# A transformer kernel re-sequenced: mixer gates, the squares of the norms, attention's early passes, and the SGU's loads and variance

## The chip, the cores and the metric

The kernel runs on one core of one Trainium2 chip. A core has five engines that run at the same time, each through its own list of instructions in order: TensorE (PE, matrix products), VectorE (DVE), ScalarE (ACT), GpSimd (POOL) and SyncE (SP, which issues transfers here). They wait for each other on semaphores. The metric is device time in microseconds (us); lower is better.

## What is computed

Two stacks of layers, 1024 wide, one after the other on 512 tokens (528 in the first, with 16 extra ones):

```python
for l in range(2):                        # first stack, T = 528
    h = h + hybrid_mixer(rmsnorm(h, g), w_in[l], ..., w_out[l])
    h = h + conv_glu_ffn(rmsnorm(h, g), w_up[l], ..., w_down[l])
x = rmsnorm(h, final_norm_g)[:, 16:]
for i in range(2):                        # second stack, T = 512
    x = x + 0.5 * swiglu_ffn(rmsnorm(x, ...), ...)
    h = rmsnorm(x, mix_norm[i])
    x = x + (diff_attention(h) if i == 0 else chunked_sgu(h))
    x = x + 0.5 * swiglu_ffn(rmsnorm(x, ...), ...)

# hybrid_mixer: one input projection (26 column tiles of 128), three branches
o_hg  = rmsnorm(hgrn2(hq, hf, hi)) * silu(hg)            # 4 heads of 128
o_ret = groupnorm(retention(rq, rk, rv)) * silu(rg)      # 256 wide
o_lru = rg_lru(conv(lx)) * gelu(ly)                      # 256 wide
out   = concat(o_hg, o_ret, o_lru) @ w_out
# chunked_sgu (the gMLP): the layer norm is over the 2048 columns of v
u, v = split(gelu(h @ w_in + b_in)); v = layernorm(v)
s = w_s (8 groups, 128 x 128, causal) @ v + b_s;  out = (u * s) @ w_out + b_out
```

Everything is float32.

## The kernel before

Each float32 product is made of three fast ones (fp32r): high part by high part, low by high, high by low. Activations lie transposed in SBUF (128 features by T tokens). A projection is a list of **slabs** of weights: SP loads a slab as `raw`, ACT rounds it to `whigh` (line 774), POOL subtracts to get `wlow` (line 760), and PE multiplies. PE writes output tiles alternately into two slots of PSUM (`big`); semaphores `first_half` and `slab_done` say that a tile of slot 0 or 1 is done, `tile_out` that DVE has emptied it. All orders are written out by hand, engine by engine.

**Output projections** end in `residual()` (lines 1525 to 1560): for each of 8 output tiles, DVE adds the slot to `h` (line 1547 or 1544), makes the low part of the next layer's input (`low_of`, line 1457; its high part is ACT's, line 827), and adds the tile's squares (from ACT's Square, line 799) to `acc` for the next norm (`add_squares`, line 1407). The `final` norm has a second sum, `acc2`.

**The mixer** runs the HGRN2 in 9 half-chunks u; beside each, PE does a tile of the input projection (`tile(18 + u)`), `apply(u)`, `scores(u + 1)`, `to_tokens(u + 1)`, and after each second one `out_turn`. The gates are tiles 18 and 19 (`ret_gate`), 20 to 23 (`hg_gate`) and 24, 25 (`lru_gate`). ACT's Silu and Gelu need another function table than its exponentials (line 962), so each costs a table load. After the loop comes the first pass `outa` of the output projection, over the retention and LRU parts: its operand is `xhigh` (ACT, `operand_high`, line 1093) and `xlow` (DVE, `operand_low`, line 1886). The second pass `outb` is over the HGRN2 heads. The FFN follows.

**Attention** goes through units by half-steps h. From h = 48 on the first pass of its output projection, over the first EARLY heads, is woven in (`early_steps`): PE does 3 heads' steps per half-step (2 late on), and DVE's `partial_tile` (line 1513) adds a finished tile to `h` in the half-step after it. `outb` does the other heads.

**The gMLP** has phases gv and gu (v and u tiles), then token mixing `mix` (PE, line 2778) on the normalised `vtok`. POOL's queue begins gv with two transfers (lines 751, 754: `wraw`, `bs`). The variance is 8 ACT squares (line 1258) of v minus its mean, at u tiles 1 and 2; then DVE's root (`token_roots`, lines 1422 to 1430) and `token_norm` (line 2096), four operations per quarter.

## Time and profile before

| | |
|---|---|
| Time, median of 3 runs | 3527.51 us (3524.79 to 3528.49) |
| The profiled execution: its time, its span | 3526.83 us, 3525.0 us |
| PE busy | 3430.8 us, 97% |
| DVE, POOL, ACT busy | 1665.1, 1338.8, 1171.6 us |
| PE's granted clock, mean | 0.990 |
| HBM read | 290.93 MB |

The profiled execution lies 1.8 us outside its span (launch and end), and 0.7 us below the median. Busy times say how long an engine held an instruction; they overlap. A wait in the trace is written behind the instruction that it delays, with the idle time and what ended it.

### The profile page before, as it was taken

How to read it: one execution, taken by the hardware profiler on the slowest of the kernel's cores; microseconds unless marked ns; L12 is line 12 of the kernel's file. 1: busy time of each engine (PE TensorE's matmuls, PEld its weight loads, DVE VectorE, ACT ScalarE, POOL GpSimd, SP SyncE). 2: the span in 40 equal slices, each digit the busy share in tenths (PEclk: the TensorE clock that was granted, in tenths of full speed). 3: DMA queues.
4: the chain of work that ended last, by engine and by line, in shares of the span. 5: the costliest groups of instructions: out<-in, count | busy, mean ns of one | idle time of the engine just before them, and what ended most of it. 6: DMA issues, size and time to landing. Idle time of an engine off the chain costs nothing.

```text
span 3525.0 us, 54336 instructions
## 1 busy us (share of the span) xinstructions
PE 3430.8 (97%) x20190; PEld 2973.8 (84%) x20190; DVE 1665.1 (47%) x2642; ACT 1171.6 (33%) x1986; POOL 1338.8 (38%) x530
## 2 busy tenths in 40 slices
PE   7999999989989999999999989999999999999999
PEld 6998999989989898788877768888888877888887
DVE  5476534544765255532546754245423523734242
ACT  2465323324653233222235432222222234322122
POOL 3312443423134444444432224444444433344443
PEclk9999999999999999999999999999999999999999
DMA  3212332322123333233322113333333322233333
GB/s 107 73 43 61 89 92 88 93 66 69 43 66 90 96 88 97 78 101 90 99 74 61 61 48 95 96 93 98 90 95 90 101 86 83 78 92 93 95 95 96
DMA packets 561404, 294.91 MB, mean 84 GB/s; under 512 B 10727, under 2 KB 560230, under 8 KB 561142
## 3 DMA queue, kind: packets, MB, share of 16 engines
q1 hardware_dynamic: 560084, 291.33, 28.3%
q8 instruction: 91, 1.49, 0.2%
q0 software_dynamic: 768, 1.11, 0.1%
q10 hardware_dynamic: 418, 0.62, 0.1%
q14 instruction: 43, 0.35, 0.0%
HBM read 290.93 MB, written 2.10 MB: 83 GB/s over the span
## 4 chain that ended last, share of the span: by engine, by line
PE 62%; issue 26%; POOL 7%; DVE 3%; ACT 2%; POOLq 0%; DMA 0%; SPq 0%; ACTq 0%; DVEq 0%
PE big L2181 51%; POOL wlow L760 7%; PE big L2614 3%; PE big L2222 2%; PE misc L2235 1%; PE misc L2246 0%; PE misc L2668 0%; DVE mix_lev L1673 0%; PE misc L2272 0%; DVE fresh L1649 0%; ACT whigh L774 0%; PE misc L2778 0%; PE misc L2374 0%; PE big L2702 0%; DMA load_xin<-in_x 0%
## 5 line engine op out<-in xcount | busy, mean ns | idle before, releaser
L760 POOL TENSOR_TENSOR wlow<-raw,whigh 128x1024 fp32r<-128x1024 f32 (+2 forms) x508 | 1328.6, 2615 | 2158.4 <-ACT whigh L774 2158.4
L774 ACT CAST whigh<-raw 128x1024 fp32r<-128x1024 f32 (+2 forms) x508 | 563.4, 1109 | 1915.5 <-PE big L2181 1781.1
L2181 PE MATMUL big<-ffn_x2l,whigh 128*128 128x264 f32 (+2 forms) x2016 | 539.2, 322 | 0.0
L2181 PE MATMUL big<-ffn_x2h,whigh 128*128 128x264 f32 (+2 forms) x2016 | 536.9, 320 | 2.1 <-DVE ffn_zg L1585 2.1
L2181 PE MATMUL big<-ffn_x2h,wlow 128*128 128x264 f32 (+2 forms) x2016 | 536.4, 320 | 0.0
L2181 PE MATMUL big<-xhigh,whigh 128*128 128x512 f32 (+1 forms) x1680 | 525.3, 350 | 0.7 <-POOL wlow L760 0.7
L2181 PE MATMUL big<-xlow,whigh 128*128 128x512 f32 (+1 forms) x1680 | 518.3, 346 | 0.0
L2181 PE MATMUL big<-xhigh,wlow 128*128 128x512 f32 (+1 forms) x1680 | 516.2, 345 | 0.0
L2181 PE MATMUL big<-ffn_hidl,whigh 128*128 128x512 f32 (+1 forms) x1232 | 419.8, 364 | 0.0
L2181 PE MATMUL big<-ffn_hidh,wlow 128*128 128x512 f32 (+1 forms) x1232 | 418.7, 363 | 0.0
L2181 PE MATMUL big<-ffn_hidh,whigh 128*128 128x512 f32 (+1 forms) x1232 | 417.6, 362 | 0.0
L2181 PEld LDWEIGHTS big<-ffn_x2h,whigh 128*128 128x128 f32 x2016 | 335.4, 189 | 33.0 <-DVE ffn_zg L1585 2.5
L2181 PEld LDWEIGHTS big<-ffn_x2l,whigh 128*128 128x128 f32 x2016 | 335.1, 189 | 29.5
L2181 PEld LDWEIGHTS big<-ffn_x2h,wlow 128*128 128x128 f32 x2016 | 334.9, 189 | 28.6
L2181 PEld LDWEIGHTS big<-xhigh,whigh 128*128 128x128 f32 x1680 | 293.3, 189 | 45.0 <-POOL wlow L760 2.0
L2181 PEld LDWEIGHTS big<-xlow,whigh 128*128 128x128 f32 x1680 | 291.7, 189 | 39.2 <-issue 0.2
L2181 PEld LDWEIGHTS big<-xhigh,wlow 128*128 128x128 f32 x1680 | 291.7, 189 | 39.0
L1595 DVE TENSOR_TENSOR ffn_pr<-big,rstd 128x512 f32<-128x512 f32 x88 | 60.8, 691 | 417.0 <-PE big L2181 411.4
L2181 PEld LDWEIGHTS big<-ffn_hidh,whigh 128*128 128x128 f32 x1232 | 219.4, 188 | 40.6 <-DVE ffn_hidl L1605 0.5
L2181 PEld LDWEIGHTS big<-ffn_hidl,whigh 128*128 128x128 f32 x1232 | 219.6, 188 | 39.6
L2181 PEld LDWEIGHTS big<-ffn_hidh,wlow 128*128 128x128 f32 x1232 | 220.0, 188 | 37.9
L1603 DVE CAST ffn_hidh<-ffn_pr 128x512 f32 (+3 forms) x132 | 238.2, 1805 | 17.5
(402 smaller groups left out, 4090.7 us busy)
## 6 DMA issues: line engine op xcount, KB each, us to landing
raw<-in_ffn_w_gate_up SPq DMA_DIRECT2D x176, 512.0 KB, 3.8
raw<-in_ffn_w_down SPq DMA_DIRECT2D x96, 704.0 KB, 4.5
raw<-in_ffn_w_up SPq DMA_DIRECT2D x88, 512.0 KB, 3.8
raw<-in_w_in SPq DMA_DIRECT2D x52, 512.0 KB, 3.8
raw<-in_gmlp_w_in SPq DMA_DIRECT2D x32, 512.0 KB, 4.0
raw<-in_attn_w_in SPq DMA_DIRECT2D x24, 512.0 KB, 3.7
raw<-in_w_out SPq DMA_DIRECT2D x16, 512.0 KB, 3.5
raw<-in_gmlp_w_out SPq DMA_DIRECT2D x16, 512.0 KB, 3.6
```

The lines of the kernel that those rows point to most:

```text
L760: eng.tensor_tensor(wlow[:, at0:at0 + n], raw[:, at0:at0 + n], whigh[:, at0:at0 + n].bitcast(F32), ALU.subtract).then_inc(slab_split, 1)
L774: eng.copy(whigh[:, at0:at0 + w], raw[:, at0:at0 + w]).then_inc(high_rounded, 1)
L1595: eng.tensor_tensor(pr[:, 0:T], wide(big, 1, T), rstd[:, 0:T], ALU.mult).then_inc(tile_out[1], 1)
L1603: eng.tensor_copy(c1(hidh, i, K), pr[:, 0:K]).then_inc(hidh_ready, 1)
L2181: mm = eng.matmul(wide(big, slot, T)[:, c:c + n], w[:, (s * KC + k) * P:(s * KC + k + 1) * P], x[:, (x0 + k) * width + c:(x0 + k) * width ...
L2222: mm = eng.matmul(wide(big, s, T)[:, c:c + cn], w[:, (s * KC + k) * P:(s * KC + k + 1) * P], x[:, k * width + c:k * width + c + cn], start ...
L2235: mm = eng.matmul(dst[:, col + j * heads:col + (j + 1) * heads], src[:, x0:x0 + P], square(mat)[:, 0:P:P // heads], start=True, stop=True)
L2614: mm = eng.matmul(wide(big, j % 2, T2), w[:, (j % 2 * KC + k) * P:(j % 2 * KC + k + 1) * P], x[:, k * T1:k * T1 + T2], start=k == 0 and y ...
```

## The change

Five edits, in the order of the program:

1. **Mixer.** The LRU gate's tiles are now 20 and 21, those of the HGRN2 gate 22 to 25. ACT does the Gelu of the LRU gate right behind the Silu of the retention gate (u = 5), DVE multiplies by it one half-chunk earlier, and the four operands of outa are made together before `select`. PE does slab 0 of outa whole before `out_turn(3)`, and the `apply` of the last half-chunk stands between the two tiles of slab 1.
2. **Squares.** In `residual()` the squares of tile k - 1 are added after the residual of tile k.
3. **Attention.** EARLY is 4 instead of 5, the steps are spread two and three in turn, and `partial_tile` comes in the same half-step in which PE's tile is done.
4. **gv.** POOL makes the first pair of `wlow` before the two transfers.
5. **Variance.** v tiles 0 to 7 give a shift, and four squares of that half are done beside v tiles 11 to 14; the other four at u tiles 1 and 2. DVE has seven more small operations (`token_means`, one in `token_roots`).

```diff
-MIX_COLS = [(2048, 4), (2816, 2), (512, 4), (0, 4), (1024, 4), (2560, 2), (1536, 4), (3072, 2)]
+MIX_COLS = [(2048, 4), (2816, 2), (512, 4), (0, 4), (1024, 4), (2560, 2), (3072, 2), (1536, 4)]
-EARLY = 5
+EARLY = 4
-    counts = {h: 3 if h < 60 else 2 for h in range(48, ATT_END - 1)}
+    counts = {h: 2 + (h < 60 and h % 2 == 0) for h in range(48, ATT_END - 1)}
...
+                if st.name == "gv":
+                    pair(0)
+                    eng.wait_ge(slab_done, st.base)
...
+                    repeat(eng, 1, st.slabs // 2, pair)
+                    continue
...
-                    tile(18 + u)
+                    if u < LAST - 1:
+                        tile(18 + u)
+                    else:
+                        eng.wait_ge(slab_done, s0 + MIX_TILES)
+                        leave(eng.copy(c1(hg_gate, HH - 1), wide(big, 1, T1)), MIX_TILES - 1)
+                        for j in range(4):
+                            operand_high(j)
+                        high_of(s0 + MIX_TILES + 1)
...
                     if u == 5:
-                        for i in range(2):
+                        for i in range(4):
                             tile_wait(TILE_RG + i)
                         eng.activation(ret_gate[:, :], ret_gate[:, :], ACT.Silu).then_inc(gates_ready.sem, 1)
+                        eng.activation(lru_gate[:, :], lru_gate[:, :], ACT.Gelu_apprx_tanh).then_inc(gates_ready.sem, 1)
...
+                    if 11 <= i < 15:
+                        variance(0, i - 11)
...
-                        for k in range(4):
-                            variance(4 * (i - 1) + k)
+                        variance(1, 2 * (i - 1))
+                        variance(1, 2 * (i - 1) + 1)
...
+                        if more and not (isinstance(k, int) and k == 0):
+                            sums(k - 1, 1 - s)
...
-                        if more:
-                            add_squares(norm_of[m], k, s, Tn)
...
+                def sums(k, s):
+                    add_squares(norm_of[m], k, s, Tn)
...
+                if more:
+                    sums(KD - 1, 1)
...
-                eng.wait_ge(gates_ready.sem, gates_ready.at(l, "lru"))
-                for p in range(2):
-                    eng.tensor_tensor(c1(lh, p), c1(lh, p), c1(lru_gate, p), ALU.mult).then_inc(lgated.sem, 1)
-                operand_low(0)
-                operand_low(1)
+                        eng.wait_ge(gates_ready.sem, gates_ready.at(l, "lru"))
+                        for p in range(2):
+                            eng.tensor_tensor(c1(lh, p), c1(lh, p), c1(lru_gate, p), ALU.mult).then_inc(lgated.sem, 1)
+                for j in range(4):
+                    operand_low(j)
                 select(LAST)
...
-                        if done == h - 1:
+                        if done == h:
                             partial_tile(outa, T2, j, s)
...
                 for s in range(2):
                     slot_free(s, t1 // 2)
-                    for j in range(2):
+                    for j in range(4):
                         eng.wait_ge(x_ready, qo + j + 1)
-                        out_steps(0, s, [4 + j], j == 0, False, None)
+                        out_steps(0, s, [4 + j], j == 0, j == 3, slab_done if s else first_half)
                 out_turn(3)
...
+                out_steps(1, 0, [4, 5, 6, 7], True, True, first_half)
                 apply(LAST)
-                out_slab(outa, 1, [4, 5, 6, 7])
+                slot_free(1, t1 // 2 + 1)
+                out_steps(1, 1, [4, 5, 6, 7], True, True, slab_done)
```

In the lists below (rows of registers, branches and loop control are left out), names in front of the arrow are written, those behind it read.

**ACT at the end of a mixer.** In the half-chunk before the last, before the change, ACT's list has slab and gate copies, then the Gelu of the LRU gate with its table load, and the operands in two pairs (`mix_ro` retention, `mix_lh` LRU) around the norm of the output (lines 981 and 985):

```order
L774 CAST whigh<-raw 128x1024
L927 COPY mix_lru_gate<-big 128x528
L1104 ACT_TABLE_LOAD
L1104 ACTIVATE mix_lru_gate<-mix_lru_gate 128x1056
L1093 CAST xhigh<-mix_ro 128x528 x2
L981 COPY acc<-misc 128x256
L985 ACTIVATE mix_psel,mix_osum<-acc 128x128 x2
L1093 CAST xhigh<-mix_lh 128x528 x2
```

After the change the Gelu stands earlier, beside the Silu and before the exponentials (lines 964, 965):

```order
L1123 ACT_TABLE_LOAD
L1123 ACTIVATE mix_ret_gate<-mix_ret_gate 128x1056
L1124 ACT_TABLE_LOAD
L1124 ACTIVATE mix_lru_gate<-mix_lru_gate 128x1056
L964 ACT_TABLE_LOAD
L964 ACTIVATE fresh<-fresh 128x2x64
```

and where it stood there are a copy of the last gate tile and all four operands, in one piece:

```order
L1106 COPY mix_hg_gate<-big 128x528
L1095 CAST xhigh<-mix_ro 128x528 x2
L1095 CAST xhigh<-mix_lh 128x528 x2
L776 CAST whigh<-raw 128x1024
L983 COPY acc<-misc 128x256
L987 ACTIVATE mix_psel,mix_osum<-acc 128x128 x2
```

The Gelu and one more table load have moved ahead of the exponentials of the last half-chunk, and the norm's copies now stand behind all operands and a slab.

**DVE in the outb of a mixer**, the loop over its output tiles (two tiles per round), before:

```order
L1547 TENSOR_TENSOR h<-big,h 128x528
...
L1457 SCALAR_TENSOR_TENSOR ffn_x2l<-h,par,ffn_x2h 128x528
...
L1407 TENSOR_TENSOR acc<-acc,sqr 128x528
...
L1547 TENSOR_TENSOR h<-big,h 128x528
...
L1457 SCALAR_TENSOR_TENSOR ffn_x2l<-h,par,ffn_x2h 128x528
```

and after, with the peeled first round ahead of the loop and the last sum behind it:

```order
L1406 MEMSET acc 128x528
L1551 TENSOR_TENSOR h<-big,h 128x528
L1461 SCALAR_TENSOR_TENSOR ffn_x2l<-h,par,ffn_x2h 128x528
L1551 TENSOR_TENSOR h<-big,h 128x528
L1411 TENSOR_TENSOR acc<-acc,sqr 128x528
L1461 SCALAR_TENSOR_TENSOR ffn_x2l<-h,par,ffn_x2h 128x528
...
L1411 TENSOR_TENSOR acc<-acc,sqr 128x528
```

The sum of squares (`acc`) has moved from behind its own tile's low part to between the next tile's residual and low part.

**POOL at the start of the gMLP**, before, from the last slabs of the FFN ahead:

```order
L760 TENSOR_TENSOR wlow<-raw,whigh 128x1408
...
L760 TENSOR_TENSOR wlow<-raw,whigh 128x1408
...
L751 DMA gmw_wraw<-in_gmlp_w_s 128x8x128
L754 DMA gmw_bs<-in_gmlp_b_s 128x1024
...
L760 TENSOR_TENSOR wlow<-raw,whigh 128x1024
...
L760 TENSOR_TENSOR wlow<-raw,whigh 128x1024
```

and after:

```order
L752 TENSOR_TENSOR wlow<-raw,whigh 128x1408
...
L752 TENSOR_TENSOR wlow<-raw,whigh 128x1024 x2
L758 DMA gmw_wraw<-in_gmlp_w_s 128x8x128
L761 DMA gmw_bs<-in_gmlp_b_s 128x1024
...
L752 TENSOR_TENSOR wlow<-raw,whigh 128x1024
```

The first two `wlow` of the gMLP are ahead of the two transfers, which wait for the FFN's last tile.

## Rows read from the trace of the kernel before

**Rows 1.** Waits of the whole run on PE: us in all, times, longest us

```profile
PE big L2631 <- DVE h L1513: 8.1, 4, 3.9
PE big L2561 <- DVE xlow L1886: 7.2, 2, 3.6
...
PE big L2631 <- DVE h L1547: 3.1, 6, 0.7
...
PE big L2181 <- DVE ffn_zg L1585: 2.1, 2, 1.1
...
PE big L2631 <- issue: 1.0, 1, 1.0
PE big L2561 <- DVE h L1547: 1.0, 2, 0.5
...
PE big L2181 <- POOL wlow L760: 0.7, 1, 0.7
```

**Rows 2.** Timeline of PE, attention: start us, us, [idle before <-releaser]

```profile
2033.79 0.77 PE L2631 MATMUL big<-att_oh,whigh 128*128 128x512 f32 x1 [3.88 <-DVE h L1513]
...
2096.25 0.47 PE L2222 MATMUL big<-ffn_x2h,whigh 128*128 128x512 f32 x1 [1.27 <-issue]
...
2100.87 0.50 PE L2222 MATMUL big<-ffn_x2h,whigh 128*128 128x512 f32 x1 [1.61 <-POOL wlow L760]
```

**Rows 3.** Timeline of POOL at the start of the gMLP

```profile
2838.24 0.95 POOL L751 DMA_DIRECT2D gmw_wraw<-in_gmlp_w_s  x1 [10.92 <-PE big L2181]
...
2839.75 4.68 POOL L760 TENSOR_TENSOR wlow<-raw,whigh 128x1024 fp32r<-128x1024 f32 x2
```

**Rows 4.** Timeline of PE at the start of the gMLP

```profile
2842.16 0.80 PE L2222 MATMUL big<-xhigh,whigh 128*128 128x512 f32 x1 [4.22 <-POOL wlow L760]
2842.75 0.63 PE L2222 MATMUL big<-xlow,whigh 128*128 128x512 f32 x1
2843.18 0.63 PE L2222 MATMUL big<-xhigh,wlow 128*128 128x512 f32 x1
```

**Rows 5.** Timeline of PE at the start of an ordinary SwiGLU FFN

```profile
2471.23 0.50 PE L2222 MATMUL big<-xhigh,whigh 128*128 128x512 f32 x1 [0.84 <-POOL wlow L760]
2471.57 0.40 PE L2222 MATMUL big<-xlow,whigh 128*128 128x512 f32 x1
2471.80 0.39 PE L2222 MATMUL big<-xhigh,wlow 128*128 128x512 f32 x1
```

**Rows 6.** Timeline of ACT, gMLP: the first square of the variance

```profile
2960.17 1.15 ACT L1258 ACTIVATE sqr<-gm_vtok,gmo_vstat 128x1024 f32<-128x1024 f32 x1 [0.98 <-DVE gmo_vstat L2081]
```

**Rows 7.** Timeline of DVE, gMLP: root of the variance and two normalised quarters

```profile
2972.76 2.39 DVE L1426 SCALAR_TENSOR_TENSOR rcol<-rcol 128x4 f32<-128x4 f32 x1
...
2975.97 3.82 DVE L2096 TENSOR_SCALAR gm_vtok<-gm_vtok,gmo_vstat 128x512 f32<-128x512 f32 x4
...
2980.31 1.90 DVE L2096 TENSOR_SCALAR gm_vtok<-gm_vtok,gmo_vstat 128x512 f32<-128x512 f32 x4
```

**Rows 8.** Timeline of POOL beside it

```profile
2975.77 2.37 POOL L760 TENSOR_TENSOR wlow<-raw,whigh 128x1024 fp32r<-128x1024 f32 x1 [0.64 <-ACT whigh L774]
```

**Rows 9.** Timeline of PE, gMLP: first token mixing

```profile
2979.84 2.08 PE L2778 MATMUL misc<-gmo_wt,gm_vtok 128*128 128x128 f32 x8 [5.28 <-DVE gm_vtok L2096]
```

**Rows 10.** Timeline of ACT, end of mixer 0

```profile
263.14 1.09 ACT L1121 ACTIVATE mix_ret_gate<-mix_ret_gate 128x1056 f32<-128x1056 f32 x1
264.24 1.28 ACT L962 ACT_TABLE_LOAD   x1
```

**Rows 11.** Timeline of DVE, end of mixer 0

```profile
283.54 1.33 DVE L1905 TENSOR_TENSOR mix_lh<-mix_lh,mix_lru_gate 128x528 f32<-128x528 f32 x2 [4.62 <-ACT mix_lru_gate L1104]
```

**Rows 12.** Timeline of PE: mixer 0's output projection and its FFN

```profile
285.63 0.78 PE L2561 MATMUL big<-xhigh,whigh 128*128 128x264 f32 x2 [3.62 <-DVE xlow L1886]
...
343.69 0.52 PE L2222 MATMUL big<-ffn_x2h,whigh 128*128 128x264 f32 x2 [1.49 <-POOL wlow L760]
```

**Rows 13.** Windows: PE, PEld, DVE, ACT, POOL busy (x), PEclk, DMA share, GB/s

```profile
284.00:292.00 8.00, 6.37 (x32) 6.40 (x33) 5.07 (x11) 3.32 (x12) 0.00 (x0) 0.57 0.20 66
```

More of the change, by code:

```diff
@@ L1099, in mix @@
                         eng.wait_ge(lru_step.sem, lru_step.at(l, 1, 5))
-                    tile(18 + u)
-                    if u == LAST - 1:
-                        for i in (TILE_LY, TILE_LY + 1):
-                            tile_wait(i)
-                        eng.activation(lru_gate[:, :], lru_gate[:, :], ACT.Gelu_apprx_tanh).then_inc(gates_ready.sem, 1)
-                        operand_high(0)
-                        operand_high(1)
-                    out_copy(u)
-                    if u == LAST - 1:
-                        operand_high(2)
-                        operand_high(3)
-                    tokens(u + 1)
+                    if u < LAST - 1:
[6 more added lines that the diff above has]
+                        high_of(s0 + MIX_TILES + 1)
+                    out_copy(u)
+                    tokens(u + 1)
+                    if u == LAST - 1:
+                        out_scale(3)
                     if u % 2:
@@ L1233, in gmlp @@
                 t0, q0 = tile_of[n], fill_of[n]
-                mean, part, var2 = vstat[:, 0:4], vstat[:, 8:12], vstat[:, 16:24]
+                shift, var2 = vstat[:, 8:16], vstat[:, 16:24]
                 def gelu_tile(dst, slot, bias0, i, base):
@@ L1913, in mix @@
                 out_gate(1)
+                partial_tile(outa, To, 1, 0)
                 out_root(4)
-                partial(outa, To, 1)
+                partial_tile(outa, To, 1, 1)
                 out_low(0)
@@ L2058, in gmlp @@
                 t0, q0 = tile_of[n], fill_of[n]
-                mean, part, var, rs = [vstat[:, 8 * k:8 * k + 4] for k in range(4)]
-                var2 = vstat[:, 16:24]
+                mean, sums, shift, var2 = vstat[:, 0:4], (vstat[:, 4:8], vstat[:, 28:32]), vstat[:, 8:16], vstat[:, 16:24]
+                part, rs = vstat[:, 8:12], vstat[:, 24:28]
                 def scale_tile(st, i, at):
@@ L2073, in add_term, with token_means @@
                                              op0=ALU.mult, op1=ALU.add).then_inc(addend_ready, 1)
-                def token_means():
-                    eng.wait_ge(g_tok, NG)
-                    eng.tensor_reduce(part, vsum[:, :].rearrange("p (j m) -> p j m", j=4), AX.X, ALU.add).then_inc(g_mean, 1)
-                    eng.wait_ge(g_mean, 1)
-                    eng.tensor_scalar(mean, part, -1.0 / GH, None, ALU.mult).then_inc(g_mean, 1)
-                    eng.tensor_scalar(part, part, -float(GH) ** -1.5, None, ALU.mult).then_inc(g_mean, 1)
+                def token_means(half):
+                    eng.wait_ge(g_tok, 8 * (half + 1))
+                    v = vsum[:, :].rearrange("p (j m) -> p j m", j=4)[:, :, 8 * half:8 * half + 8]
+                    eng.tensor_reduce(sums[half], v, AX.X, ALU.add).then_inc(g_mean, 1)
+                    eng.wait_ge(g_mean, 3 * half + 1)
+                    eng.tensor_scalar(shift[:, 4 * half:4 * half + 4], sums[half], -2.0 * float(GH) ** -1.5, None, ALU.mult
+                                      ).then_inc(g_mean, 1)
+                    if half == 0:
+                        eng.tensor_copy(mean, sums[0]).then_inc(g_mean, 1)
+                        return
+                    eng.tensor_tensor(mean, sums[0], sums[1], ALU.add).then_inc(g_mean, 1)
+                    eng.tensor_tensor(sums[0], sums[0], sums[1], ALU.subtract).then_inc(g_mean, 1)
+                    eng.wait_ge(g_mean, 7)
+                    eng.tensor_scalar(mean, mean, -1.0 / GH, None, ALU.mult).then_inc(g_mean, 1)
+                    eng.tensor_tensor(sums[1], sums[0], sums[0], ALU.mult).then_inc(g_mean, 1)
@@ L2083, in token_roots @@
                 def token_roots():
                     eng.wait_ge(g_var, 8)
-                    eng.wait_ge(g_mean, 3)
-                    v2 = var2.rearrange("p (j x) -> p j x", x=2)
-                    eng.tensor_tensor(part, v2[:, :, 0], v2[:, :, 1], ALU.add).then_inc(g_root, 1)
+                    eng.wait_ge(g_mean, 9)
+                    eng.tensor_tensor(part, var2[:, 0:4], var2[:, 4:8], ALU.add).then_inc(g_root, 1)
                     eng.wait_ge(g_root, 1)
+                    eng.scalar_tensor_tensor(out=part, in0=sums[1], scalar=float(GH) ** -2, in1=part,
+                                             op0=ALU.mult, op1=ALU.add).then_inc(g_root, 1)
@@ L2131, in gmlp @@
                         add_term(2 * (i - 4) + 1)
+                    if i == 10:
+                        token_means(0)
                 eng.wait_ge(addend_ready, NG)
```

54 lines of the change are left out of this document (24 added, 30 removed).

## The prediction, made before the changed kernel ran

> **What bounds the kernel now.** I read the busy times first: PE holds an instruction for 97% of the span, and no edit adds or removes a matmul of any size. So the change can only gain what PE waits, and what it loses to a lower clock after a wait. Next comes the list of PE's waits by what ended them [rows 1]: the reader is to see that those which the edits touch are small. Then the timelines of PE around the longest of them, and of the engine that ended each. Last, the matmuls behind a long wait: at the gMLP's start they follow each other at 0.43 us [rows 4], against 0.23 us for the same matmul in an ordinary FFN [rows 5]. That is TensorE at the lower of its two clocks (1.2 of 2.4 GHz). A wait of 3 us or more on PE thus costs its length and some 2 to 3 us behind it; shorter ones mostly cost their length.
>
> **Attention and its FFN's start: -10.8 us (-6 to -14).** Waits for the residuals in this part are 8.1 us in 4 waits (line 1513, partial sums of the first pass), 1.0 us in one, and 3.1 us in 6 (line 1547) [rows 1]; with 1.27 and 1.61 at the FFN's first tiles [rows 2] that is 15.1 us. Two more are lost at the low clock behind the longest (3.88 us) [rows 2]: about ten matmuls of 512 columns at 0.43 instead of 0.23 us. After the change, four heads' steps instead of five make a tile, and DVE empties the slot in the half-step in which it is filled, so PE comes back to the slot with a half-step in between where it had none. I followed the semaphores through h = 48 to 64: six waits are left, of about 0.6, 0.6, 0.3, 2.85, 0.4 and 0.7 us, 5.5 in all. The long one is the residual of slot 1 at h = 54, which stands in DVE's order behind `combine` and `out_root`. That takes some 8.8 us off up to the end of outb (its six waits of 0.5 us stay at roughly a third, since the sum of squares, next paragraph, leaves the chain), and 2.0 at the FFN, where the second slab's subtraction comes earlier and an ordinary FFN's 0.84 us [rows 5] is left in place of 1.27 + 1.61. The ends: if two of the six are longer than I read them, -6; if the 2.85 us does not come, -14.
>
> **Squares one tile later: in the terms of each FFN start.** In an output loop the chain for a slot is PE's tile, DVE's residual, ACT's high part (0.9 us), DVE's low part, and then the squares, 0.7 us, ahead of the next residual. The edit puts them in the 0.9 us in which DVE waits for ACT anyway. No work is added. At the two mixers the waits that go are 0.5 us each in outb (1.0 in 2 on line 1547 [rows 1], and as much on "issue"), most of the 1.49 us behind POOL [rows 12], and the 1.1 us at the FFN's first gate (2.1 in 2, line 1585 [rows 1]). I take -2.9 and -3.0, **-5.9 us** in all (-3 to -6). At the starts of norms that wait on `acc` the last sum is where it was: 0 (0 to +0.7).
>
> **gv: -6.1 us (-5 to -6.5).** POOL waits for the last tile of the FFN before, issues two transfers, 2838.24 to 2839.75, and only then subtracts twice (4.68 us) [rows 3]; PE waits 4.22 us for the first [rows 4]. An ordinary FFN with its `wlow` ready waits 0.84 us [rows 5]. That is 3.4 us. Then about twelve matmuls at 0.43 instead of 0.23, 2.4 to 2.7 us more. The transfers land about 4 us later and are needed some 15 us after the start, so they stay hidden; if they didn't, PE would wait about 1 us.
>
> **Token mixing: -6.9 us (-1.9 to -8.2).** The first mixing waits 5.28 us [rows 9], and a tile just before it 0.7 [rows 1]; the low clock behind it costs 2.2 us (eight small matmuls at double time and six large ones). The wait is the sum of ACT's eight squares from 2960.17, of 1.15 us and the read of their sum, 1.3 each [rows 6], the root, and four normalisations [rows 7]. Four squares move to v, 5 us off ACT's chain; the seven new DVE operations are 0.2 us each, and six of them lie in idle time. Not all 5.3 us go, since DVE is held up twice here. A small root operation takes 2.39 us and four normalisations 3.82, against 1.90 for four a little later [rows 7], and each time POOL's subtraction, 2.37 us, starts in the same moment [rows 8]. One such hold-up stays in my reading, and about 1.3 us of wait. The Trainium skill says in "SBUF — State Buffer", section "Who interferes with whom", that VectorE and GpSimd share a port pair and whoever issues first holds it for its whole instruction; the trace agrees (2.39 us beside 2.37). By that rule alone, whether the next subtraction catches the last normalisation is decided by about 0.4 us, and this is the first rival.
>
> **Mixer ends: 0 us (-8 to +6, both mixers).** Before, outa's first matmul waits 3.62 us [rows 12] for the Gelu, the gating [rows 11] and the operands, and the clock in 284 to 292 is 0.57 [rows 13]: 3.6 us and some 2.8 more per mixer. In the new order the Gelu (1.09, as the Silu) and a table load (1.28) [rows 10] lie ahead of the exponentials of the last half-chunk, and the gating of 1.33 us [rows 11] ahead of its DVE work. That chain, exponentials, state, copies for the tokens, `apply`, has PE waiting for it: 2.4 + 1.3 = 3.7 us later, in three waits of about 2.1, 1.3 and 0.3. PE thus reaches outa at 285.5 instead of 285.63, now without a wait. The gain is the low clock, if three shorter waits do not bring it as well; the Silu of the HGRN2 gate comes at the same time as before and bounds outb's start, so that I find at most 0.9 us at each mixer, and 1.7 to 2.7 us of loss if the clock falls again. I take 0. The ends: the 3.7 us all hidden, -4 each; all exposed behind the old bound, +3 each. In "ScalarE: Activation LUTs", section "What ACT_TABLE_LOAD costs", the Trainium skill adds a drain of 1380 ns to the 1283 ns of a table load; here the load starts 0.01 us after the activation ahead of it ends and takes 1.28 [rows 10], so that the trace does not show it. By the page the estimate would be 2.8 us slower in all.
>
> **Sum.** -10.8 - 5.9 - 6.1 - 6.9 + 0 = -29.7 us. The profiled execution took 3526.8, 0.7 below the median of 3527.5; so 3497.1 on its own scale and 3497.8 on the median's. I say 3497.
>
> **Rivals.**
> - *The port.* DVE's last normalisation falls behind a second subtraction (2.4 us), the mixing waits 4.1 us and the low clock stays: the term is -1.9 instead of -6.9, 3502. The same at the output loops: a pair of tiles needs 4.7 us of DVE and, with a subtraction in it, 7.1, against 6.1 us of PE; the twelve slabs of three such loops lose up to 1.0 each: 3509. For it: both held-up operations in [rows 7]. Against it: PE waits only 0.5 us per tile in such loops now [rows 1]. Chance 0.2.
> - *The mixers lose.* The new waits bring the low clock before outa; +3 each and the FFN starts at the small end (-3): 3506. For it: the clock falls behind shorter waits too (the 0.57 of [rows 13] lasts longer than the wait). Chance 0.12.
> - *The mixers gain.* ACT has slack that I have not seen, and neither wait nor clock loss is left: -4 to -7 each, 3484 to 3489. Chance 0.1.
> - *The waits move only.* In attention DVE's order, not PE's slots, sets the pace; attention gives 4, the others half: 3527 - 15 = 3512. Chance 0.06.
> - *Slower.* One mechanism at the mixers: PE has nothing to do while the exponentials wait for Gelu and table, so the whole 3.7 us is exposed, and the clock stays low from there through outa, 24 us of work at half rate, up to 12 us: 15.7 each, 31 in both, 3528. It decides from 15 us per mixer on. Against it: in [rows 13] the low clock went after 6 us. Chance 0.02.
>
> The forecast has 0.5. A difference of 0.2%, 7 us, is about what a measurement of this kernel can tell from none. Faster by more than that: all cases but the last and the tail of the one before, 0.94; within it 0.04; slower 0.02. The range is that of the terms and takes in the port, the losing mixers and most of the gaining ones: 3484 to 3512.
>
> **What would show it.** Right: PE's waits on line 1517 (the new number of 1513) below 5 us in all, one of them near 2.9; the gMLP's first wait below 1 us with matmuls 0.23 apart behind it; the first mixing's wait at 1 to 2 us; no wait over 0.5 at outa, but three ahead of it. Wrong: a clock below 0.7 in 262 to 292, a mixing wait of 4 us with POOL's subtraction beside the last normalisation, low parts or residuals in outb that take 2 us and more one after another, or waits of PE in attention that keep their sum and change their name.

## The result and the profile after

The changed kernel takes 3507.73 us (median of 5 runs, 3507.09 to 3513.93) against 3527.35 us before: ratio 0.9951, 95% interval 0.994 to 0.9963, 19.6 us less. The forecast was 3497, 30 us less, with 3484 to 3512 as range. Time and sign lie inside it, but a third of the gain is missing, and the terms are off by more than the sum. The profiled execution took 3507.73 us, its span 3505.9; the spans of the two profiled executions differ by 19.1 us. The same marks of PE in both traces (the ends of waits that both have) divide that:

| mark (us) | before | after | gained since the last |
|---|---|---|---|
| first wait in mixer 0's half-chunk 6 | 256.78 | 256.00 | 0.8 |
| second slab of the FFN behind mixer 0 | 343.69 | 339.97 | 2.9 |
| the same wait in mixer 1 | 959.61 | 956.07 | -0.2 |
| second slab of the FFN behind mixer 1 | 1044.34 | 1039.48 | 1.3 |
| attention, last wait before the first pass | 1842.22 | 1837.56 | -0.2 |
| second slab of the FFN behind attention | 2100.87 | 2094.19 | 2.0 |
| second slab of the next FFN | 2471.23 | 2464.67 | -0.1 |
| end of the wait at the first token mixing | 2979.84 | 2962.61 | 10.7 |
| second slab of the last FFN | 3150.78 | 3131.69 | 1.9 |

The 0.8 us at the top are the first load, which ended earlier in that execution. The gMLP gives 10.7 + 1.9, the mixers 4.2, attention 2.0.

Such a stretch is exact for its two executions, but PE's clock falls in some executions of the same code and not in others, and each time that moves a mark by about 1.6 us. Two falls of this kind are in the table. The trace of the kernel before has a low clock right behind the first mark (0.52 in 257 to 260), which b_squares, with the same code there, has not (1.00): 1.6 of the mixers' 4.2 us are that. In attention it is the other way round. In 2045 to 2050 the clock of the kernel before is 1.00, but it fell there in the traces of c_mixer and d_gmlp, whose attention is the same code, and they take 630.6 us from attention's last wait to the second slab of the next FFN, where the kernel before takes 629.0. Against them attention gains 3.5 us, not 1.9.

The list of PE's waits after, in us in all, times and longest, with the rows that answer to [rows 1]:

```profile
PE big L2243 <- POOL wlow L752: 10.8, 8, 2.0
PE misc L2416 <- issue: 8.8, 6, 3.2
PE big L2652 <- DVE h L1517: 8.5, 4, 4.6
...
PE misc L2799 <- DVE gm_vtok L2115: 1.5, 1, 1.5
```

The 7.2 us on outa's operands are gone, and 5.3 at the token mixing are 1.5. But the partial sums of attention (line 1517, before 1513) are 8.5 us in 4 waits, where they were 8.1, and the mixers' line on "issue" has come up from 2.7 to 8.8. So PE waits for attention's partial sums as long as before. Its timeline there, against [rows 2]:

```profile
2036.31 0.47 PE L2652 MATMUL big<-att_oh,whigh 128*128 128x512 f32 x1 [2.03 <-DVE h L1517]
...
2045.70 0.80 PE L2652 MATMUL big<-att_oh,whigh 128*128 128x512 f32 x1 [4.55 <-DVE h L1517]
...
2064.40 0.51 PE L2652 MATMUL big<-att_oh,whigh 128*128 128x512 f32 x1 [1.61 <-DVE h L1517]
...
2094.19 0.50 PE L2243 MATMUL big<-ffn_x2h,whigh 128*128 128x512 f32 x1 [2.04 <-POOL wlow L752]
```

What DVE did ahead of each is in its timeline, and below it is POOL's for the same stretch:

```profile
2032.70 2.86 DVE L1448 TENSOR_TENSOR att_ol<-fresh,att_oh 128x512 fp32r<-128x512 f32 x1
...
2041.48 2.19 DVE L1427 TENSOR_SCALAR rcol<-rcol 128x4 int32<-128x4 int32 x1
...
2060.65 2.12 DVE L1429 TENSOR_TENSOR rcol<-rcol 128x4 f32<-128x4 f32 x1
```

```profile
2032.25 2.76 POOL L752 TENSOR_TENSOR wlow<-raw,whigh 128x1024 fp32r<-128x1024 f32 x1 [16.05 <-ACT whigh L776]
...
2041.31 2.34 POOL L752 TENSOR_TENSOR wlow<-raw,whigh 128x1024 fp32r<-128x1024 f32 x1 [6.30 <-ACT whigh L776]
...
2058.03 4.72 POOL L752 TENSOR_TENSOR wlow<-raw,whigh 128x1024 fp32r<-128x1024 f32 x2 [14.38 <-ACT whigh L776]
```

Three operations that take 0.68, 0.17 and 0.16 us elsewhere take 2.86, 2.19 and 2.12, and each ends where a subtraction of POOL ends (2032.25 + 2.76 = 2035.01, the DVE operation 2035.56 with 0.6 of its own; 2041.31 + 2.34 = 2043.65, the operation 2043.67; 2058.03 + 4.72 = 2062.75, the operation 2062.77). That is the hold-up of [rows 7, 8], in a stretch (2029 to 2072) in which the kernel before has none of it.

The gMLP, PE's timeline and then DVE's and POOL's, against [rows 4, 7, 9]:

```profile
2835.12 0.50 PE L2243 MATMUL big<-xhigh,whigh 128*128 128x512 f32 x1 [0.95 <-POOL wlow L752]
...
2962.61 1.16 PE L2799 MATMUL misc<-gmo_wt,gm_vtok 128*128 128x128 f32 x8 [1.46 <-DVE gm_vtok L2115]
```

```profile
2956.82 2.40 DVE L1427 TENSOR_SCALAR gmo_vstat<-gmo_vstat 128x4 int32<-128x4 int32 x1
...
2960.64 1.92 DVE L2115 TENSOR_SCALAR gm_vtok<-gm_vtok,gmo_vstat 128x512 f32<-128x512 f32 x4
...
2962.36 2.43 POOL L752 TENSOR_TENSOR wlow<-raw,whigh 128x1024 fp32r<-128x1024 f32 x1 [3.16 <-ACT whigh L776]
```

gv now begins without a wait, and its second slab waits 0.95 us, about as in every FFN. At that slab (2847.45 before, 2835.12 after) the two terms can be told apart: gv gives 5.8 us, the mixing 6.8. At the mixing one root operation is held up (2.40), the four normalisations are not (1.92), and PE waits 1.46 us.

The mixer's end, PE and ACT, against [rows 10, 12]:

```profile
271.01 0.66 PE L2416 MATMUL misc<-squares_sb,mix_v 128*128 128x128 f32 x2 [3.22 <-issue]
...
284.27 0.49 PE L2582 MATMUL big<-xhigh,whigh 128*128 128x264 f32 x2
```

```profile
264.41 1.08 ACT L1124 ACTIVATE mix_lru_gate<-mix_lru_gate 128x1056 f32<-128x1056 f32 x1
...
265.51 1.28 ACT L964 ACT_TABLE_LOAD   x1
```

Instead of the forecast three waits of 3.7 us in all there is one of 3.22, ahead of `to_tokens`. Outa starts at 284.27 without a wait, and the clock of 284 to 292 is not low, but it falls behind the new wait:

```profile
284.00:292.00 8.00, 8.00 (x68) 8.00 (x67) 3.83 (x8) 4.31 (x14) 2.40 (x1) 1.00 0.21 66
270.00:275.00 5.00, 3.99 (x22) 4.02 (x23) 3.72 (x15) 3.33 (x13) 2.36 (x1) 0.66 0.14 32
```

(The columns are those of [rows 13].) In mixer 0 the low clock has moved ahead of outa and is shorter there; in mixer 1 it has moved as well, and is as long as before (0.66 in 987 to 992 before and in 970 to 975 after).

### The profile page after: what moved, and what is told of

It is laid out like the page before. It is cut to its first block, busy times and chain, and to the rows that moved or that the text cites. A ratio compares the mean times of both kernels' runs of the same rounds, so it can differ in the third digit from the quotient of the medians.

```text
span 3505.9 us, 54254 instructions
## 1 busy us (share of the span) xinstructions
PE 3420.9 (98%) x20190; PEld 2965.9 (85%) x20190; DVE 1669.8 (48%) x2649; ACT 1171.2 (33%) x1986; POOL 1348.9 (38%) x530
## 3 DMA queue, kind: packets, MB, share of 16 engines
q8 instruction: 91, 1.49, 0.2%
## 4 chain that ended last, share of the span: by engine, by line
PE 61%; issue 29%; POOL 7%; DVE 2%; ACT 1%; POOLq 0%; DMA 0%; SPq 0%; DVEq 0%; ACTq 0%
PE big L2202 51%; POOL wlow L752 7%; PE big L2635 3%; PE big L2243 2%; PE misc L2256 1%; PE misc L2267 0%; PE misc L2689 0%; PE misc L2293 0%; PE misc L2799 0%; PE big L2723 0%; ACT whigh L776 0%; DVE fresh L1492 0%; PE misc L2307 0%; DVE acc L1411 0%; DMA load_xin<-in_x 0%
## 5 line engine op out<-in xcount | busy, mean ns | idle before, releaser
L752 POOL TENSOR_TENSOR wlow<-raw,whigh 128x1024 fp32r<-128x1024 f32 (+1 forms) x508 | 1338.7, 2635 | 2140.1 <-ACT whigh L776 2140.1
L776 ACT CAST whigh<-raw 128x1024 fp32r<-128x1024 f32 (+1 forms) x508 | 563.5, 1109 | 1907.4 <-PE big L2202 1776.9
```

Of the source, the lines that this page charges most:

```text
L752: eng.tensor_tensor(wlow[:, at0:at0 + n], raw[:, at0:at0 + n], whigh[:, at0:at0 + n].bitcast(F32), ALU.subtract).then_inc(slab_split, 1)
L776: eng.copy(whigh[:, at0:at0 + w], raw[:, at0:at0 + w]).then_inc(high_rounded, 1)
```

## The experiments

Twelve kernels ran, each beside the kernel before, whose median was between 3527.2 and 3528.4 in the same sessions. The changed kernel itself was timed only in its own session. "Against the changed kernel" thus compares sessions, and its interval (0.994 to 0.9963) touches or overlaps those of all the runs built on it but e_short, l_cut and m_cutnosq: a difference of a few us is not shown by the medians alone.

| run | edit | median us | ratio to before, 95% |
|---|---|---|---|
| a_att | before + attention edit | 3521.39 | 0.9984 (0.9974 to 0.9993) |
| b_squares | before + squares edit | 3532.04 | 1.0015 (1.0005 to 1.0024) |
| c_mixer | before + mixer edit | 3524.09 | 0.999 (0.9981 to 1.0) |
| d_gmlp | before + both gMLP edits | 3514.82 | 0.9965 (0.9953 to 0.9978) |
| e_short | after, short subtractions in attention | 3499.71 | 0.992 (0.9903 to 0.9937) |
| f_casts | after, roundings re-placed | 3504.12 | 0.9935 (0.9919 to 0.9952) |
| g_rootlast | after, partial sum ahead of the root | 3508.23 | 0.9946 (0.9929 to 0.9962) |
| h_castfirst | after, last rounding first | 3507.98 | 0.9942 (0.9926 to 0.9959) |
| j_nosq | after - squares edit | 3508.46 | 0.9945 (0.9928 to 0.9962) |
| k_best | j + f + g | 3502.06 | 0.9929 (0.9912 to 0.9945) |
| l_cut | after, short subtractions in second passes | 3492.82 | 0.9907 (0.9891 to 0.9924) |
| m_cutnosq | l - squares edit | 3493.49 | 0.9904 (0.9887 to 0.992) |

### The edits one by one

```diff
-EARLY = 5
+EARLY = 4
...
-                        if done == h - 1:
+                        if done == h:
```

> The kernel before with the attention edit alone (EARLY 4, steps two and three in turn, partial_tile in the same half-step). My theory, the port: POOL's subtractions of the output projection's slabs now start beside DVE operations that they hold up by about 2.2 us each, in the att_ol subtraction near h = 52 and twice in out_root; so this edit by itself brings 0 to -2 us (about 3526) and those three DVE operations take 2 to 3 us. Rival, the new order works as I had worked it out and something in the other edits spoils it: -8 to -9 us here (about 3518), with every DVE operation at its usual length.

> The kernel before with the squares edit alone. If the sum of squares is out of the slot's chain and nothing takes its place, the waits on the residuals in the three output loops go and -3 us comes in all from the two mixers and 2 from attention. With the port theory every second low part takes 2.5 us instead of 0.77, and the wait for the FFN's second subtraction grows from 1.5 to 1.9 us: -1 us per loop, -3 in all, 3524.

> The kernel before with the mixer edit alone. The wait of 3.6 us ahead of outa goes and one of 3.2 us for the state of the last half-chunk comes: 0 to -1 us per mixer, 3526. Rival, the two mixers' gain in the changed kernel (4.2 us) is this edit's and not the squares': -4 us, 3523.

> The kernel before with the two gMLP edits (subtractions ahead of the transfers, variance in two halves) alone. Both terms as in the changed kernel: -12.6 us, 3515, with no matmul at 0.43 us pitch at the start of gv or behind the first mixing. Rival: part of that gain needs the other edits (the phase of slabs and transfers): less than 10.

The four effects are -6.5, +4.2, -3.8 and -13.1 us on their own medians, -19.2 in all, beside 19.6 for the whole change. That they add up is partly chance: without the squares edit the other three make -23.4, and the kernel that has just these three (j_nosq, below) gains 18.7.

**a_att** came out between the two theories, and by its time (-2.5 to -9.2 us) the rival's -8 would be possible. Its trace has the hold-ups at the first and the last place (2.86 and 2.10 us), so that the rival is out, but not the one in the middle. As I read it the reason is PE's clock. After the same wait of 2.03 us it fell here and not in the changed kernel (PE's timeline and then the window behind the wait in a_att, and the window behind the same wait, at 2036.31, in the changed kernel; PEclk is the third column from the right):

```profile
2040.83 0.47 PE L2631 MATMUL big<-att_oh,whigh 128*128 128x512 f32 x1 [2.03 <-DVE h L1513]
```

```profile
2041.00:2046.00 5.00, 5.00 (x24) 4.69 (x24) 3.10 (x8) 1.63 (x4) 0.00 (x0) 0.61 0.31 103
```

```profile
2036.00:2041.00 5.00, 4.70 (x29) 4.02 (x29) 3.13 (x8) 2.82 (x6) 0.00 (x0) 1.00 0.38 105
```

With PE at half rate, ACT's copy and its rounding came later, POOL's subtraction began at 2047.67, behind the root instead of in it, and the 4.55 us wait is missing (timelines of POOL and DVE in a_att):

```profile
2047.67 2.39 POOL L760 TENSOR_TENSOR wlow<-raw,whigh 128x1024 fp32r<-128x1024 f32 x1 [8.14 <-ACT whigh L774]
...
2046.00 0.17 DVE L1423 TENSOR_SCALAR rcol<-rcol 128x4 int32<-128x4 int32 x1
...
2047.46 0.68 DVE L1513 TENSOR_TENSOR h<-big,h 128x512 f32<-128x512 f32 x1
```

So a fall of the clock saved the next, longer wait. The other traces bear this out. Behind the same wait of 2.03 us the clock fell in l_cut and m_cutnosq too (0.57 and 0.59 over 5 us), and neither has the long wait; it did not fall in h_castfirst and j_nosq (1.00), and both have it, 4.54 and 4.55. (It fell in g_rootlast as well, 0.55, but there DVE's order is another one.) From the same mark to the next FFN's second slab (1842 to 2466) a_att takes 624.2 us, and j_nosq, with the same code there, 627.2.

**b_squares** is the surprise: slower, and beyond what either theory had. The hold-ups are there, DVE and POOL in attention's second pass:

```profile
2081.78 2.34 DVE L1407 TENSOR_TENSOR acc<-acc,sqr 128x512 f32<-128x512 f32 x1
...
2087.60 2.27 DVE L1407 TENSOR_TENSOR acc<-acc,sqr 128x512 f32<-128x512 f32 x1
...
2094.36 2.47 DVE L1457 SCALAR_TENSOR_TENSOR ffn_x2l<-h,par,ffn_x2h  x1 [0.34 <-ACT ffn_x2h L827]
```

```profile
2081.72 1.85 POOL L760 TENSOR_TENSOR wlow<-raw,whigh 128x768 fp32r<-128x768 f32 x1 [7.27 <-ACT whigh L774]
...
2087.47 1.85 POOL L760 TENSOR_TENSOR wlow<-raw,whigh 128x768 fp32r<-128x768 f32 x1 [3.90 <-ACT whigh L774]
...
2093.43 2.85 POOL L760 TENSOR_TENSOR wlow<-raw,whigh 128x1024 fp32r<-128x1024 f32 x1 [4.10 <-ACT whigh L774]
```

ACT makes the high part, the square and the rounding of the next slab in one go, so POOL starts a little after each pair of tiles. In the old order the residual lay there, which reads one operand from PSUM and was not held up, and the 0.9 us in which DVE waits for ACT (DVE and POOL in the kernel before):

```profile
2080.32 0.69 DVE L1547 TENSOR_TENSOR h<-big,h 128x512 f32 x1
...
2080.17 1.92 POOL L760 TENSOR_TENSOR wlow<-raw,whigh 128x768 fp32r<-128x768 f32 x1 [7.37 <-ACT whigh L774]
```

With the sum moved, DVE has a sum (2.34, 2.27) or a low part (2.47) there in every round. But that alone is not the 4 us. PE's six waits of 3.1 us in the second pass are now three of 2.7, and the pass is 0.4 us shorter; the FFN's second slab then waits 2.04 us for POOL instead of 1.61. What follows is the clock, PE's window behind that slab in b_squares and, behind a wait of the same 2.04 us, in the changed kernel:

```profile
2103.00:2107.00 4.00, 4.00 (x12) 3.15 (x11) 0.67 (x2) 0.00 (x0) 0.00 (x0) 0.57 0.45 131
...
2094.00:2098.00 4.00, 3.81 (x21) 3.29 (x22) 1.29 (x2) 0.00 (x0) 0.14 (x1) 1.00 0.44 131
```

The fall costs 1.7 us. The clocks of all executions say the same: in b_squares's ten the mean is 0.988, in the 27 of the kernel before it is 0.990. The share that is missing to 1, times the span, is the most that a low clock can cost: 42.0 and 35.7 us, 6.3 us apart, where the medians are 4.2 apart. So all or most of its loss is one of clock. Which of its waits brings the falls is not shown, since the changed kernel has the same hold-ups in its second passes and loses nothing by the edit.

**c_mixer** gives -3.8 us, with an interval that reaches 0. It is nearer to the rival (-4) than to my 0 to -1 for each mixer, but it doesn't settle what the squares edit adds there: with the chance fall of the clock taken out the mixers' stretches of the changed kernel give 2.6 us, and those of c_mixer's trace, which has falls of its own, 2.1. **d_gmlp** is as forecast.

### Is it the port, and how much?

```diff
-                        at0, n = s * KC * P, st.kc * P
+                        at0, n = s * KC * P, 8 if st.name in ('aouta', 'aoutb') else st.kc * P
```

> The changed kernel, but POOL subtracts only 8 of the 1024 columns of each slab of attention's output projection (its low parts are left out of the product, so the output is not the reference's). Port theory: no DVE operation in 2024 to 2090 is held up any more (att_ol 0.7, root operations 0.2), the waits of 2.0, 4.6 and 1.6 us shrink to 0, about 2.4 and 0, the low clock behind the longest goes: -6 to -8 us against the changed kernel. Rival, DVE's order (out_root ahead of the partial sum) sets the waits: -1 us or less and the 4.6 us stays above 4.

PE's work is the same in this run; it multiplies by what `wlow` held before. It gives -8.0 us against the changed kernel, and 10.3 in the stretch from attention's last wait ahead of the first pass (1840.74) to the second slab of the next FFN but one (2457.56). In the first pass the hold-ups are gone and one wait of 2.45 us is left of the three; in the second, two low parts are still held up (2.33 and 2.43 us) by the subtractions for the FFN (timelines of DVE and of PE in e_short):

```profile
2034.83 0.69 DVE L1448 TENSOR_TENSOR att_ol<-fresh,att_oh 128x512 fp32r<-128x512 f32 x1
...
2041.44 0.17 DVE L1427 TENSOR_SCALAR rcol<-rcol 128x4 int32<-128x4 int32 x1
```

```profile
2043.64 0.51 PE L2652 MATMUL big<-att_oh,whigh 128*128 128x512 f32 x1 [2.45 <-DVE h L1517]
```

The 2.45 us are the partial sum behind the root, which I had worked out as 2.85 before the change ran; the clock did not fall behind them (1.00 in 2043 to 2048). The rival is out as the cause of the other two waits and of 2.1 of the 4.55 us; the order of DVE's work sets the rest.

### Can it be had with all the work done?

```diff
+                    if h == EARLY_DONE[0, 1] + 1:
+                        high_of(outa.base + 2)
...
+                    if h == EARLY_DONE[2, 1] + 1:
+                        high_of(outb.base)
...
-                        if EARLY_DONE[j, 1] == h - 1:
-                            high_of(outa.base + j + 2)
+                    if h == EARLY_DONE[1, 1] + 1:
+                        eng.wait_ge(tile_out[1], (t0 + 24) // 2 + 2)
+                        high_of(outa.base + 3)
+                    if h == EARLY_DONE[3, 1] + 1:
+                        eng.wait_ge(aorstd, AH)
+                        high_of(outb.base + 1)
```

> The changed kernel with ACT's four roundings in attention's output projection moved so that POOL's subtractions fall into DVE's idle time: the first ahead of the exponentials, the second and the fourth behind a wait for the partial sum and for out_root, the third ahead of out_head. All work is done. Port theory: as e_short, -5 to -8 us against the changed kernel. Rival: less than -1 us, since the hold-ups only ran beside a wait that stays; or the later slabs make PE wait for POOL and give back 2 us.

-3.6 us, and 4.7 in attention's stretch. All four executions (3502.9 to 3504.6) are faster than all five of the changed kernel. POOL's four subtractions take 2.37 or 2.38 us each. Behind the last three DVE's operations keep their usual time, so three of the four placings work, and the first does not (timelines of POOL, DVE and PE in f_casts):

```profile
2030.85 2.38 POOL L752 TENSOR_TENSOR wlow<-raw,whigh 128x1024 fp32r<-128x1024 f32 x1 [13.11 <-ACT whigh L776]
...
2046.08 2.37 POOL L752 TENSOR_TENSOR wlow<-raw,whigh 128x1024 fp32r<-128x1024 f32 x1 [12.85 <-ACT whigh L776]
...
2031.13 2.10 DVE L2000 TENSOR_TENSOR att_top<-att_top,att_alpha 128x2 f32<-128x2 f32 x1
```

```profile
2034.83 1.13 PE L2696 MATMUL misc<-att_kt,att_qt 64*128 64x512 f32 x4 [1.00 <-ACT att_ex L1177]
...
2037.59 0.47 PE L2659 MATMUL big<-att_oh,whigh 128*128 128x512 f32 x1 [0.74 <-DVE h L1524]
...
2044.97 0.50 PE L2659 MATMUL big<-att_oh,whigh 128*128 128x512 f32 x1 [2.52 <-DVE h L1524]
```

The first subtraction holds up the operation that the exponentials wait for (2.10 instead of 0.16 us, both end at 2033.23), and PE's 1.00 us behind them is the price of that. 2.52 is the wait behind the root, here with a low clock behind it (0.66 in 2045 to 2050), and the four hold-ups in the second pass (2.42 to 2.55 us), of which e_short has two, stay.

```diff
+                    for (j, s), done in EARLY_DONE.items():
+                        if done == h == 54:
+                            partial_tile(outa, T2, j, s)
...
-                        if done == h:
+                        if done == h != 54:
```

> The changed kernel with the partial sum of h = 54 ahead of out_root in DVE's order. Port theory plus order: the 4.6 us wait falls by the root (1.7 us and the 2.0 us of its hold-up, 3.7 in all) to under 1 us, the low clock behind it goes, and the root's end delays the following head a little: -3 to -5 us against the changed kernel. Rival: the wait moves to what waits for out_root, 0.

The median is the changed kernel's, 0.5 us over it. The trace has no wait over 2.1 us in this pass, but the clock fell behind the one of 2.03, as in a_att (PE's timeline, and the window behind it):

```profile
2039.58 0.47 PE L2655 MATMUL big<-att_oh,whigh 128*128 128x512 f32 x1 [2.03 <-DVE h L1517]
```

```profile
2040.00:2045.00 5.00, 5.00 (x24) 4.62 (x22) 3.16 (x7) 1.63 (x4) 0.00 (x0) 0.55 0.25 87
```

I can't tell from one trace how much of the order's gain this took; from 1841 to 2466 it is 1.6 us faster, with one more fall of the clock behind the FFN's second slab (0.57 in 2095 to 2099) that costs 1.6 us. The gain of 3 to 5 us is not there in the time.

```diff
+                    if j == st.slabs - 1:
+                        high_of(st.base + j + 2)
                     after_residual(n, 2 * j, 0, tile0 // 2 + j + 1)
-                    high_of(st.base + j + 2)
+                    if j < st.slabs - 1:
+                        high_of(st.base + j + 2)
```

> The changed kernel with ACT's rounding of the FFN's second slab ahead of the high part of output tile 6 instead of behind its square, in all three output loops with a split. The wait of 1.9 to 2.0 us at the FFN's first gate comes from POOL's subtraction, which starts at the end of a chain that DVE's held-up low part delays: it falls to 0.3 us or less, -1.6 us in each of three places, -5 us against the changed kernel. Rival: the next wait (the low parts of tiles 6 and 7) takes its place, less than -1.

No change that can be measured. POOL's waits at the three FFNs (1.93, 1.93 and 2.04 us) are gone, and waits of 1.58, 1.43 and 1.32 us stand in their place: the subtraction now holds up the low part of tile 6, which delays the residual of tile 7 and so the free slot (timelines of PE, DVE and POOL in h_castfirst):

```profile
341.94 0.48 PE L2246 MATMUL big<-ffn_x2h,whigh 128*128 128x264 f32 x2 [1.58 <-issue]
...
338.98 2.24 DVE L1464 SCALAR_TENSOR_TENSOR ffn_x2l<-h,par,ffn_x2h  x1 [1.26 <-ACT ffn_x2h L829]
...
338.27 2.39 POOL L752 TENSOR_TENSOR wlow<-raw,whigh 128x1024 fp32r<-128x1024 f32 x1 [2.35 <-ACT whigh L776]
```

### What is the squares edit worth?

> The changed kernel with the squares edit taken back (the sum of squares behind its own tile's low part again), all else as changed. From the run with that edit alone (+4 us, of which 3.5 in attention's second pass and its FFN start) I expect the squares edit to cost 2 to 4 us here too: 3504 to 3506, the gain in attention and nearly none at the mixers. Rival: the squares edit pays once the others are in: 3508 to 3510.

> The changed kernel, but POOL subtracts only 8 columns of each slab of the second passes of the output projections (two mixers, attention) and of the first two slabs of the FFNs behind them; these low parts are left out, so the output is not the reference's. Port theory for the squares edit: the low parts of 2.5 us fall to 0.77, the FFN's wait for POOL (1.9, 1.9 and 2.0 us) goes, about -5 to -6 us against the changed kernel. Rival: PE's tile time sets these loops anyway and the FFN's start waits for something else: -1 or less.

> The same cut of POOL's subtractions, in the changed kernel without the squares edit. Beside the run with the cut and with the edit this shows what moving the squares is worth when the port is free: by my prediction's reasoning this one is 2 to 4 us slower than that one (residual waits of 0.4 to 0.6 us per tile in the second passes come back). Rival: no difference, the edit is worth nothing even then.

```diff
+                        if st.name in ('m0outb', 'm1outb', 'aoutb') or (st.name in ('c0u0', 'c1u0', 'f0u0') and isinstance(i, int)):
+                            n = 8
...
```

Taking the edit back in the changed kernel gives 3508.46, 0.7 us more; its four executions lie 2 to 3 us to either side of that, so it tells nothing. With the port free it is the same: 3492.82 with the edit, 3493.49 without. In attention the traces are finer, since the clock took the same course in each pair: 627.1 and 627.2 us from the last wait to the next FFN but one, and 616.9 and 617.8 with the port free. So I find no more than about 1 us for the edit there, and my 2 to 4 us for the residual waits that it takes out was wrong even without the port. Why it costs 4 us by itself (b_squares) and nothing in company stays open.

The cut itself is large: 14.9 us between the changed kernel and l_cut, more than the 5 to 6 that I expected. Its trace gives 2.5 and 2.8 us to the mixers' ends and 10.2 to attention, where this run has no wait over 0.9 us behind the one of 2.03. Attention's first pass was not cut in it; the 4.55 us wait is missing as in a_att, where this course of the clock was worth 3.0 us (624.2 for 627.2). The changed kernel's waits behind that point, six of 6.1 us in all (1.00, 1.61, 0.50, 0.57, 0.42 and 2.04), are gone with the cut. By these two estimates 6 to 7 of the 10.2 us come from the shorter subtractions.

### All together

> The changed kernel without the squares edit, with the four roundings of attention's output projection re-placed and the partial sum of h = 54 ahead of out_root. If the three effects add (3 for the squares, 4.7 for the roundings in attention's stretch, 1.7 for the wait of 2.5 us that then is left): 3498, and no wait over 1 us in attention's first pass. Rival: the root's delay comes back at the next head: 3500 to 3502.

3502.06 us: 5.7 less than the changed kernel, 6.4 less than j_nosq in the same session, and all its executions (3500.7 to 3504.1) are faster than those of both kernels. 3498 would have been the sum. The rival is nearer, and the trace shows its form: the wait for the partial sum, behind which the second rounding stands, ends earlier now, so that POOL catches the root again (timelines of DVE and POOL in k_best):

```profile
2045.32 2.26 DVE L1440 SCALAR_TENSOR_TENSOR rcol<-rcol 128x4 f32<-128x4 f32 x1
...
2045.19 2.37 POOL L752 TENSOR_TENSOR wlow<-raw,whigh 128x1024 fp32r<-128x1024 f32 x1 [11.20 <-ACT whigh L776]
```

The waits behind it are 0.9 and 0.7 us instead of 2.5, since the partial sum is through before.

## Why the prediction was right, and where it was not

- **gMLP, both terms (-6.1 and -6.9): right.** Forecast -13.0; the stretches give -5.8 and -6.8, and the edits alone -13.1. The wait at the mixing was put at 1.3 and is 1.46, with one hold-up, as read from [rows 7]. The first rival, a second subtraction that catches the last normalisation, did not happen: POOL's next subtraction starts at 2962.36, when the last of the four, which end at 2962.56, was already running. With about 0.5 us for each, the margin was 0.3 us; I had estimated 0.4.
- **Attention (-10.8): the step that failed** is "I followed the semaphores through h = 48 to 64: six waits are left [...] 5.5 in all". I followed them with DVE's operations at their usual lengths. The four subtractions of POOL were moved by the same edit (four heads per slab, other half-steps), from DVE's idle time into its work, and I had not placed them. Without them the stretch gives 12.2 us against the kernel before (616.8 for 629.0 from attention's last wait ahead of the first pass to the next FFN but one, in e_short); with them, 1.9. That bears out the order of the work that I had planned, but not the 10.8 as such, since e_short also takes out most of the second pass's subtractions, which my term left in. The port was among the rivals with 0.2. It had the gMLP, where the second hold-up did not come, and the output loops, where it did (low parts of 2.3 to 2.6 us, and 14.9 us less in l_cut, not all of it the port's); the first pass of attention, where it cost most, it had not.
- **Squares (-5.9 with the FFN starts): wrong.** The step that failed is "The edit puts them in the 0.9 us in which DVE waits for ACT anyway", taken to be free. It is the time in which POOL starts. Most of the 1.49 us of the FFN's second wait was to go, and it rose to 1.93. But even with the port free no more than about 1 us shows, so the residual waits are worth less than their sum; why is not shown.
- **Mixer ends (0): mis-sized.** The chain and the time of arrival were right (one wait of 3.22 for three of 3.7, no wait at outa, 284.3 against 285.5 forecast). The clock did fall ahead of outa, as the forecast feared (0.66 in 270 to 275), but less than it had at outa. The term is -2.6 us by the stretches without the chance fall, -3.8 by c_mixer, where I took 0. Whether and how far the clock falls there could not be read from the trace before, and I had set the gain against the fear.
- **The clock: the rule was too narrow.** "A wait of 3 us or more on PE thus costs its length and some 2 to 3 us behind it" held for the waits that it was read from, of 3.6 to 5.3 us. But the clock fell behind a wait of 2.03 us in four of seven traces, and behind the FFN's second slab (waits of 1.76 to 2.04 us) in b_squares, e_short and g_rootlast and not in the changed kernel.
- **The signs.** Those of gv, of the mixing and of outa's start came as forecast. Three of those for being wrong came as well: 8.5 us on line 1517 instead of less than 5, low parts of over 2 us in every second tile of outb, and the clock of 270 to 275.
- **The sum**: -2.0 - 4.2 - 12.6 and 0.8 of the load are -19.6, and the small stretches between give 0.5 back, which makes the 19.1 of the two spans. The errors of attention (+8.8), squares (+5.9) and mixers (-4.2, of which 1.6 are chance) partly cancel. That the time lies in the range is thus in part luck, though the range had been made to take in the port.

What stays open: the five runs of the changed kernel lie at 3507.1 to 3507.7 (three) and at 3512.5 and 3513.9. The mean granted clock does not tell them apart (0.994 once, 0.991 or 0.992 otherwise). The two courses in attention (clock low behind 2.03, or a wait of 4.55) differ by 3 us, but they are not the answer by themselves: the one trace of the changed kernel has the slower course and is one of the three of 3507 us.

## What to carry to other kernels

When an edit moves the work of VectorE, write down where GpSimd's long operations will then stand, as carefully as its own: an idle gap of VectorE may be the cover of a GpSimd operation, and what fills it may then wait for the rest of that operation. Place the instruction that triggers GpSimd (here ACT's rounding) behind the VectorE work on the critical chain, by a wait if need be: that gave 3.6 us for no work, with three of four subtractions well placed. And a change of several edits can be right in time and wrong in its parts, so time the edits alone, and in company: one of these costs 4 us by itself and nothing in company. Before a stretch of one trace is read to a microsecond, look at the granted clock in it: a fall that the same code has in one execution and not in the next is worth 1.6 us here.

## What was not expected of the hardware

- GpSimd is held up as well. Behind a VectorE operation on two SBUF operands that has just begun, its subtraction of 1024 columns takes 2.89 us instead of 2.40, and the next VectorE operation then 2.51 instead of 0.77 (timelines of DVE and POOL in the changed kernel, second pass of mixer 0):

```profile
324.26 0.70 DVE L1411 TENSOR_TENSOR acc<-acc,sqr 128x528 f32<-128x528 f32 x1
...
325.28 2.51 DVE L1461 SCALAR_TENSOR_TENSOR ffn_x2l<-h,par,ffn_x2h  x1 [0.32 <-ACT ffn_x2h L829]
...
324.34 2.89 POOL L752 TENSOR_TENSOR wlow<-raw,whigh 128x1024 fp32r<-128x1024 f32 x1 [3.50 <-ACT whigh L776]
```

  The Trainium skill's "SBUF — State Buffer", section "Who interferes with whom", has whoever issues first hold the pair for its whole instruction; the trace agrees in both directions (0.5 us and 1.7 us).
- The size of the operation that waits does not matter: one on 4 columns (0.17 us alone) took 2.19 us, and one on 512 columns (0.68 alone) took 2.86, so that both waited 2.0 to 2.2 us for POOL.
- A wait of 2.03 us at the same place was followed by a lower clock of PE in four traces (0.55 to 0.61 over the 5 us behind it) and not in three (1.00), among them pairs with the same code in attention, and a drop can shorten the run by what it moves behind it.
